# Block owners planned ahead of the places, and the first pair's expert weights issued in another order

## The chip, the cores and the metric

The kernel runs on one core of one Trainium2 chip. The metric is the device time of one execution in microseconds (us). Of several executions the median counts, and a change is judged against the kernel before on the same chip.

## What is computed

The program is a chain of two blocks over 256 tokens of width 1024. The first is a two-layer mixer with a feed-forward network; the second is a mixer followed by a mixture of experts. Only the end of the second block matters here:

```
lg = tok @ rt_g + rt_g_b;  grp = argmax(lg)             # one of 4 groups for each token
le = tok @ rt_e + rt_e_b;  top 2 of the 8 experts in that group
order = argsort(e_flat); counts, starts, padded blocks  # the plan: which expert owns which block
def expert_block(idx, w, e):
    xb = tok_pad[idx]
    hb = silu(xb @ ex_gate[e]) * (xb @ ex_up[e])
    return (hb @ ex_down[e]) * w[:, None]
out = zeros.at[tok_buf].add(y);  x = layernorm(ALPHA * x + g2 * out)
```

There are 32 experts. Each has an input matrix pair (gate and up, 1024 by 512, 2048 KB each) and an output matrix (down, 512 by 1024, 2048 KB), all float32. Which experts are needed, and in what order, is known only once the router has run.

## The kernel before, in words

Each engine has its own program, written out by hand, and the engines meet through semaphores. TensorE is PE, VectorE is DVE, ScalarE is ACT, and SP issues the transfers. The places of the expert blocks are groups of PLACES = 64 token slots. Owned blocks are worked in pairs. There are at most PAIRS = 20 of them, and the loop body runs only for pairs that hold a block.

**Tail** (`tail_vector`, `tail_tensor`, `tail_sync`). DVE routes both token tiles (`route`). As soon as the first tile is routed, the expert of token 0 is known (line 2996), and SP issues that expert's three matrices (line 2746) into the buffers of the pair's second half. PE counts the tokens of every expert (lines 2813 to 2820) and turns the normalised tokens (line 2826); ACT copies them out (line 2872). Then `plan` on DVE works out, from line 3031 to 3050, how many blocks each expert needs, where its blocks end and where they start. From line 3054 on it works out, for both token tiles, the place of each token's two choices (`K.place`, lines 3056 to 3065).

**First block** (`pair_vector`, `pair_tensor`, the part ahead of the loop). One block, that of token 0's expert, is computed while the weights of the first pair are on their way. On DVE this order is written out: `choose` marks the tokens of the first block (lines 3288 and 3292, event `one_chosen`), `owners` computes which expert owns each of 40 blocks (lines 3074 to 3082, event `planned`), `route_weights` works out the routing weights (lines 3013 to 3019), and `weigh` puts them into the block (lines 3302 and 3307). PE waits for `one_chosen`, gathers the block's tokens (line 3126), takes the products with up and gate (lines 3135 and 3136), gathers the first pair's tokens (line 3117), and takes the product with down (line 3160) and the products that put the block's result back on its tokens (line 3169).

**Pair weights** (`pair_sync`). SP waits for `planned`, reads the number of blocks, and in a loop over the pairs reads the two owners and issues six transfers, two gate and up pairs and two down matrices:

```
for unit, sources in (("pair_in", ...), ("pair_down", ...)):
    for j, e in enumerate(experts):
        sp.wait_ge(K.used_up((unit, j)), K.free_count((unit, j), i))
```

[...] Half 0 of a pair lies in three slots of the weight ring, which are free by then. Half 1 lies in three buffers of its own in the arena, and these are the ones that the first block reads: its input matrices until line 3136 is done, its down matrix until line 3160 is done. That there is one buffer set for each half, and no more, ties each transfer to the products of the pair before.

**Loop on PE.** For each pair: input products of half 0, then of half 1 (lines 3184 and 3185), the turned hidden values (line 3196), output products of half 0 (line 3208), the next pair's gather (line 3117), output products of half 1 (line 3208), the rest of the gather, and the products that put the results back (line 3239).

Of the kernel before, what the change touches and what calls it, by code (L numbers as in the profile page):

```python
# [19 lines left out]
P = 128  # L20
# [1369 lines left out]
EXPERTS, GROUPS_E, PER_GROUP, D_EXPERT = 32, 4, 8, 512  # L1390
# [100 lines left out]
PLACES = 64  # L1491
TOP = 2
BLOCKS = (TOP * T + EXPERTS * (PLACES - 1)) // PLACES
PAIRS = -(-BLOCKS // 2)
# [1406 lines left out]
def tail_vector(dve, K):  # L2901
# [47 lines left out]
    for tt in range(TT):  # L2949
        route(dve, K, link, tt)  # L2950
    plan(dve, K, link)
    K.dve_base = link.base + link.n

# [53 lines left out]
def route_weights(dve, K, link, tt):  # L3007

    tt_op, ts_op = dve.tensor_tensor, dve.tensor_scalar
    s = K.rt_s[:, tt, :]  # L3010
    dve.wait_ge(K.sem["rt_e2"], K.count("rt_e2", 0, tt + 1))

    ts_op(s[:, 4:5], s[:, 1:2], 1.0, None, ALU.add).then_inc(link.sem, 1)
    dve.wait_ge(link.sem, link.count())
    tt_op(s[:, 4:5], s[:, 4:5], s[:, 0:1], ALU.mult).then_inc(link.sem, 1)
    dve.wait_ge(link.sem, link.count())
    dve.reciprocal(s[:, 4:5], s[:, 4:5]).then_inc(link.sem, 1)
    dve.wait_ge(link.sem, link.count())
    tt_op(s[:, 5:6], s[:, 4:5], s[:, 1:2], ALU.mult).then_inc(link.sem, 1)
    dve.wait_ge(link.sem, link.count())  # L3020


def plan(dve, K, link):

    tt_op, ts_op, stt = dve.tensor_tensor, dve.tensor_scalar, dve.scalar_tensor_tensor
    dve.wait_ge(K.full(("pos", 0)), K.full_count(("pos", 0)))
    dve.wait_ge(K.full(("total", 0)), K.full_count(("total", 0)))

    total, its = K.bank(("total", 0))[:, 0:EXPERTS], K.bank(("pos", 0))[:, EXPERTS:2 * EXPERTS]
    blocks, ends, first, apart = (K.plan[:, k, :] for k in range(4))  # L3030
    ts_op(blocks, total, 0.0, None, ALU.is_gt).then_inc(link.sem, 1)
    dve.wait_ge(link.sem, link.count())
    for k in range(1, T // PLACES):
        ins = stt(out=blocks, in0=total, scalar=float(k * PLACES), in1=blocks, op0=ALU.is_gt, op1=ALU.add)
        if k < T // PLACES - 1:
            ins.then_inc(link.sem, 1)
            dve.wait_ge(link.sem, link.count())
        else:
            ins.then_inc(K.empty(("total", 0)), 1)
            dve.wait_ge(K.empty(("total", 0)), K.drained_count(("total", 0)))  # L3040
    tt_op(blocks, blocks, its, ALU.subtract).then_inc(link.sem, 1)
    dve.wait_ge(link.sem, link.count())
    dve.tensor_tensor_scan(ends, K.ones[:, 0:EXPERTS], blocks, 0.0, ALU.mult, ALU.add).then_inc(link.sem, 1)
    dve.wait_ge(link.sem, link.count())

    tt_op(first, ends, blocks, ALU.subtract).then_inc(link.sem, 1)
    dve.wait_ge(link.sem, link.count())
    stt(out=apart, in0=first, scalar=-float(PLACES), in1=its, op0=ALU.mult, op1=ALU.mult).then_inc(link.sem, 1)
    dve.wait_ge(link.sem, link.count())
    stt(out=first, in0=first, scalar=1.0, in1=its, op0=ALU.add, op1=ALU.subtract).then_inc(link.sem, 1)  # L3050
    dve.wait_ge(link.sem, link.count())
    for tt in range(TT):
        dve.wait_ge(K.full(("pos", tt)), K.full_count(("pos", tt)))
        pos = K.bank(("pos", tt))[:, 0:EXPERTS]
        t = K.ended[:, 0, :]
        stt(out=K.chosen[:, tt, :], in0=first, scalar=float(PLACES), in1=pos, op0=ALU.mult, op1=ALU.add).then_inc(link.sem, 1)
        stt(out=t, in0=pos, scalar=float(PLACES), in1=apart, op0=ALU.is_lt, op1=ALU.mult).then_inc(K.empty(("pos", tt)), 1)
        dve.wait_ge(link.sem, link.count())
        dve.wait_ge(K.empty(("pos", tt)), K.drained_count(("pos", tt)))
        tt_op(K.chosen[:, tt, :], K.chosen[:, tt, :], t, ALU.add).then_inc(link.sem, 1)  # L3060
        dve.wait_ge(link.sem, link.count())
        for k in range(TOP):
            tt_op(t, K.chosen[:, tt, :], K.rt_hot[:, tt, 1 + k, :], ALU.mult).then_inc(link.sem, 1)
            dve.wait_ge(link.sem, link.count())
            dve.tensor_reduce(K.place[:, tt, k:k + 1], t, AX_X, ALU.add).then_inc(link.sem, 1)
            dve.wait_ge(link.sem, link.count())


def owners(dve, K, link):

    tt_op, ts_op = dve.tensor_tensor, dve.tensor_scalar
    ends = K.plan[:, 1, :]
    n = 2 * PAIRS
    tt_op(K.ended, K.token[:, 0:n].unsqueeze(2).broadcast_to([P, n, EXPERTS]), ends.unsqueeze(1).broadcast_to([P, n, EXPERTS]),
          ALU.is_ge).then_inc(link.sem, 1)
    dve.wait_ge(link.sem, link.count())
    dve.tensor_copy(K.owner[:, n:n + 1], ends[:, EXPERTS - 1:EXPERTS])
    dve.tensor_reduce(K.owner[:, 0:n], K.ended, AX_X, ALU.add).then_inc(link.sem, 1)
    dve.wait_ge(link.sem, link.count())
    ts_op(K.owner[:, 0:n], K.owner[:, 0:n], float(EXPERTS - 1), None, ALU.min).then_inc(link.sem, 1)  # L3080
    dve.wait_ge(link.sem, link.count())
    dve.tensor_copy(K.block_expert[:, 0:n + 1], K.owner[:, 0:n + 1]).then_inc(K.sem["planned"], 1)


def pair_sync(sp, K, A):

    sp.wait_ge(K.sem["planned"], K.count("planned"))
    blocks = block_count(sp, K)
    with sp.Fori(0, PAIRS) as i, sp.If(i * 2 < blocks):
        experts = [sp.value_load(K.block_expert[0:1, bass.ds(i * 2 + j, 1)], min_val=0, max_val=EXPERTS - 1) for j in range(2)]  # L3090
        for unit, sources in (("pair_in", (A["ex_gate_2"], A["ex_up_2"])), ("pair_down", (A["ex_down_2"],))):
            for j, e in enumerate(experts):
                sp.wait_ge(K.used_up((unit, j)), K.free_count((unit, j), i))
                sp.sem_inc(K.sync_steps, 1)
                for a, dst in zip(sources, K.pair_w[unit, j]):
                    k = a.shape[2] // P
                    weights = a[0, bass.ds(e, 1)].rearrange("a (p k) n -> p (a k) n", k=k)
                    sp.dma_start(dst.rearrange("p (k n) -> p k n", k=k), weights).then_inc(K.landed((unit, j)), 16)


def block_count(eng, K):

    eng.wait_ge(K.sem["planned"], K.count("planned"))
    return eng.value_load(K.block_expert[0:1, 2 * PAIRS:2 * PAIRS + 1], min_val=1, max_val=BLOCKS)
# [179 lines left out]
def choose(dve, K, link, at, n, done):  # L3284

    slots = K.token[:, at:at + n]
    for tt in range(TT):
        ins = dve.tensor_scalar(K.hit[:, tt, 0, 0:n], slots, K.place[:, tt, 0:1], None, ALU.is_equal)
    ins.then_inc(link.sem, 1)
    dve.wait_ge(link.sem, link.count())  # L3290
    for tt in range(TT):
        ins = dve.scalar_tensor_tensor(out=K.chosen_at[:, tt, 0:n], in0=slots, scalar=K.place[:, tt, 1:2], in1=K.hit[:, tt, 0, 0:n],
                                       op0=ALU.is_equal, op1=ALU.add)
    ins.then_inc(K.sem[done], 1)
# [31 lines left out]

def pair_vector(dve, K):
    link = Chain(K.place_done)
    choose(dve, K, link, 0, PLACES, "one_chosen")
    more = Chain(K.dve_done, K.dve_base)  # L3330
    owners(dve, K, more)
    for tt in range(TT):
        route_weights(dve, K, more, tt)
    K.dve_base = more.base + more.n
# [30 lines left out]
    blocks = block_count(dve, K)  # L3365
    with dve.Fori(0, PAIRS) as i, dve.If(i * 2 < blocks):
        link = Chain(K.place_done, FIRST_LINKS, i, PLACE_LINKS)
# [326 lines left out]
def program(nc, A, out):  # L3694
# [7 lines left out]
    with ExitStack() as ctx:  # L3702
# [19 lines left out]
        @block.sync  # L3722
        def _(sp):
            for tt, landed in enumerate((K.dma_x, K.dma_x_2)):
                sp.dma_start(K.x_tok[:, tt, :], A["x"][0, tt * P:(tt + 1) * P, :]).then_inc(landed, 16)
            layer_sync(sp, K, A)
            mid_sync(sp, K, A)
            tail_sync(sp, K, A)
            pair_sync(sp, K, A)
            for tt in range(TT):  # L3730
                sp.wait_ge(K.sem["x5"], K.count("x5", 0, tt + 1))
                sp.dma_start(out[0, tt * P:(tt + 1) * P, :], K.x_tok[:, tt, :]).then_inc(K.dma_out, 16)
            sp.wait_ge(K.dma_out, 32)
# [55 lines left out]
```

## Time and profile before

| | us |
|---|---|
| median of 3 runs | 2050.88 (2049.94 to 2054.84) |
| the profiled execution, its own time | 2051.53 |
| its span, first to last instruction | 2049.3 |
| share of the span in which PE is busy | 97% |
| mean granted clock of PE | 0.985 of 2.4 GHz |

The span is read from the first to the last instruction, and times in the rows below are counted from its start. A busy PE is one with a matmul in its pipeline. "Granted clock" is the share of 2.4 GHz that the chip gave PE; 0.50 is 1.2 GHz. A line of idle time names who ended it. The tail runs to about 1576 us, the first block from there to 1607 us, and 14 pairs from there to 2031 us; the last layer norm and the store of the output end the program.

### The profile page before, as it was taken

The numbers are of one execution on the slowest core, as the hardware profiler recorded it, in microseconds if no ns is written. First come the engines' busy times: TensorE is split into PE (matmuls) and PEld (weight loads), VectorE is DVE, ScalarE is ACT, GpSimd is POOL, SyncE is SP. The second block draws the span as 40 slices with busy tenths as digits, with TensorE's granted clock in tenths as the row PEclk, the third lists the DMA queues.
The fourth block names the chain that finished last, engine by engine and source line by source line (L and its number), as shares of the span: only waits on it lengthen the run. The fifth ranks groups of instructions, "written<-read, shape, count | busy, mean of one in ns | idle before, by whom it ended". The sixth has DMA issues, their size and how long they took to land.

```text
span 2049.3 us, 35729 instructions
## 1 busy us (share of the span) xinstructions
PE 1987.9 (97%) x14735; PEld 1371.6 (67%) x14735; DVE 1097.6 (54%) x1847; ACT 477.9 (23%) x902; POOL 250.5 (12%) x233
## 2 busy tenths in 40 slices
PE   8999999999999999999999999999997999999996
PEld 5778869964867868994445565999975444444442
DVE  2685276753569157665578757444547323323324
ACT  3165110001436311000331144433233110111011
POOL 4684000000667100000000011000000000000000
PEclk9999999999999999999999999999996999999998
DMA  8332535554533355536622245100014999999992
GB/s 252 124 124 103 205 124 168 162 195 122 182 123 124 107 201 165 165 126 251 242 82 82 82 149 180 44 4 4 4 46 160 400 414 414 422 413 413 422 413 112
DMA packets 138707, 385.51 MB, mean 188 GB/s; under 512 B 16935, under 2 KB 64399, under 8 KB 127441
## 3 DMA queue, kind: packets, MB, share of 16 engines
q1 hardware_dynamic: 138577, 383.61, 50.4%
q8 instruction: 102, 1.67, 0.3%
q14 instruction: 28, 0.23, 0.0%
HBM read 382.54 MB, written 1.05 MB: 187 GB/s over the span
## 4 chain that ended last, share of the span: by engine, by line
PE 90%; ACT 4%; DVE 4%; issue 2%; DMA 0%; DVEq 0%; SPq 0%; ACTq 0%
PE psum L408 17%; PE psum L666 12%; PE psum L1609 10%; PE psum L3184 9%; PE psum L2352 8%; PE psum L3208 5%; PE psum L709 5%; PE psum L3117 3%; PE psum L426 3%; PE psum L3239 2%; PE psum L725 2%; PE psum L629 2%; PE psum L642 1%; PE psum L1814 1%; ACT arena L1979 1%
## 5 line engine op out<-in xcount | busy, mean ns | idle before, releaser
L408 PE MATMUL psum<-arena,ring 128*128 128x256 f32 x1728 | 382.3, 380 | 1.0 <-ACT arena L776 1.0
L408 PEld LDWEIGHTS psum<-arena,ring 128*128 128x128 f32 x1728 | 324.0, 189 | 55.4 <-issue 8.2
L2352 PE MATMUL psum<-arena 64*64 64x64 f32 (+1 forms) x4320 | 179.9, 237 | 2.7 <-issue 1.5
L2352 PEld LDWEIGHTS psum<-arena 64*64 64x64 f32 x4320 | 171.7, 134 | 4.7 <-issue 2.7
L666 PE MATMUL psum<-arena,ring 128*128 128x128 f32 x1280 | 149.6, 275 | 0.3 <-issue 0.2
L666 PEld LDWEIGHTS psum<-arena,ring 128*128 128x128 f32 x1280 | 146.1, 192 | 0.6 <-issue 0.6
L1609 PE MATMUL psum<-arena,ring 128*128 128x512 f32 (+2 forms) x432 | 142.2, 489 | 0.0
L776 ACT ACTIVATE arena<-psum 128x512 f32<-128x512 f32 (+2 forms) x84 | 44.7, 558 | 380.9 <-PE psum L408 163.0
L1609 PEld LDWEIGHTS psum<-arena,ring 128*128 128x128 f32 (+1 forms) x432 | 80.6, 187 | 61.4 <-issue 55.8
L666 PE MATMUL psum<-arena 128*128 128x128 f32 x960 | 113.7, 274 | 0.0
L666 PEld LDWEIGHTS psum<-arena 128*128 128x128 f32 x960 | 110.4, 192 | 0.0
L3323 DVE TENSOR_TENSOR arena<-psum,arena 64x512 f32<-64x512 f32 x58 | 40.0, 689 | 120.1 <-PE psum L3208 115.3
L2521 ACT ACTIVATE arena<-psum 128x256 f32<-128x256 f32 (+1 forms) x156 | 68.4, 446 | 141.5 <-PE psum L2352 52.9
L3184 PE MATMUL psum<-ring,arena 128*64 128x512 f32 x224 | 99.1, 595 | 0.0
L3185 PE MATMUL psum<-ring,arena 128*64 128x512 f32 x224 | 99.1, 595 | 0.0
L3373 DVE TENSOR_TENSOR arena<-arena,psum 64x512 f32<-64x512 f32 x28 | 19.0, 679 | 149.1 <-ACT arena L3265 149.1
L3185 PE MATMUL psum<-arena 128*64 128x512 f32 x224 | 98.6, 591 | 0.0
L3184 PE MATMUL psum<-arena 128*64 128x512 f32 x224 | 98.6, 591 | 0.0
L2161 DVE SCALAR_TENSOR_TENSOR arena<-psum,arena 128x189 f32<-128x189 f32 (+3 forms) x184 | 80.5, 438 | 21.6 <-ACT arena L1918 13.2
L3184 PEld LDWEIGHTS psum<-ring,arena 128*64 128x64 f32 x224 | 29.5, 137 | 66.6 <-issue 66.6
L3184 PEld LDWEIGHTS psum<-arena 128*64 128x64 f32 x224 | 30.4, 136 | 64.4 <-issue 64.4
L3265 ACT ACTIVATE arena<-psum 64x512 f32<-64x512 f32 x28 | 16.7, 595 | 230.6 <-PE psum L3185 230.6
(464 smaller groups left out, 3051.5 us busy)
## 6 DMA issues: line engine op xcount, KB each, us to landing
ring<-in_w_in_dram SPq DMA_DIRECT2D x29, 2048.0 KB, 8.1
ring<-in_ffn_w_dram SPq DMA_DIRECT2D x46, 1024.0 KB, 7.7
arena<-in_ex_gate_dram SPq DMA_DIRECT2D x15, 2048.0 KB, 11.0
arena<-in_ex_up_dram SPq DMA_DIRECT2D x15, 2048.0 KB, 15.5
arena<-in_ex_down_dram SPq DMA_DIRECT2D x15, 2048.0 KB, 14.8
ring<-in_ex_gate_dram SPq DMA_DIRECT2D x14, 2048.0 KB, 8.1
ring<-in_ex_up_dram SPq DMA_DIRECT2D x14, 2048.0 KB, 12.6
ring<-in_ex_down_dram SPq DMA_DIRECT2D x14, 2048.0 KB, 16.2
```

Source lines behind the costliest of these rows:

```text
L408: ins = pe.matmul(bank[:, j, :], w[:, kc, c * P:(c + 1) * P], moving[:, kc, :], start=kc == 0, stop=kc == k - 1)
L426: ins = pe.matmul(bank, K.xT[:, kc, tt * P:(tt + 1) * P], w[:, kc, :], start=kc == 0, stop=kc == DC - 1)
L666: ins = pe.matmul(bank[:, x, w, :], weights(w)[:, k, :], moving[:, k, :], start=k == 0, stop=k == 3)
L709: ins = pe.matmul(K.bank(key), tokens[:, k, :], weights[:, k, :], start=u == k == 0, stop=key[0] == "p" and u == BY_SEVEN - 1 and k == 1)
L1609: ins = pe.matmul(out, a, b, start=i == 0, stop=i == len(pairs_) - 1)
L2161: last = stt(out=o, in0=i, scalar=w, in1=o, op0=ALU.mult, op1=ALU.add)
L2352: ins = pe.matmul(bank[r, u, :], a[r, u], b[r, u], start=i == 0, stop=i == len(terms) - 1)
L2521: act.activation(dst, src, ACT.Copy).then_inc(K.empty(key), 1)
L3117: ins = pe.matmul(bank[:, u * P:(u + 1) * P], K.x_hat[:, tt, kc * P:(kc + 1) * P], K.chosen_at[:, tt, :], start=tt == 0, stop=tt == TT - 1)
L3184: pe.matmul(bank[0:PLACES, :], K.xg[:, kc, mine], up[:, kc, :], start=kc == 0, stop=kc == DC - 1)
L3185: ins = pe.matmul(bank[PLACES:P, :], K.xg[:, kc, mine], gate[:, kc, :], start=kc == 0, stop=kc == DC - 1)
L3208: ins = pe.matmul(bank[hf * PLACES:(hf + 1) * PLACES, :], K.p_hidT[:, j, kc, :], w[:, kc, hf * BANK:(hf + 1) * BANK], start=kc == 0, stop= ...
```

## The change

On DVE, `plan` is cut in two. Its first part (lines 3023 to 3051) stays where it was, at the end of the tail. Its second part, which computes the places, becomes a function `places`. `pair_vector` now calls `owners`, then `places`, then `choose` for the first block. No instruction of DVE is added or removed.

On SP, the first pair is taken out of the loop, and its six transfers are issued in the order input 0, output 0, input 1, output 1. The loop over the other pairs keeps its order (input 0, input 1, output 0, output 1) and starts at 1.

```diff
@@ plan(dve, K, link), after line 3051
+def places(dve, K, link):
+
+    tt_op, stt = dve.tensor_tensor, dve.scalar_tensor_tensor
+    first, apart = K.plan[:, 2, :], K.plan[:, 3, :]
     for tt in range(TT):
         dve.wait_ge(K.full(("pos", tt)), K.full_count(("pos", tt)))
         ...
@@ pair_sync(sp, K, A)
     sp.wait_ge(K.sem["planned"], K.count("planned"))
     blocks = block_count(sp, K)
-    with sp.Fori(0, PAIRS) as i, sp.If(i * 2 < blocks):
-        experts = [sp.value_load(K.block_expert[0:1, bass.ds(i * 2 + j, 1)], ...) for j in range(2)]
-        for unit, sources in (("pair_in", (A["ex_gate_2"], A["ex_up_2"])), ("pair_down", (A["ex_down_2"],))):
+
+    def owned(i):
+        return [sp.value_load(K.block_expert[0:1, bass.ds(i * 2 + j, 1)], ...) for j in range(2)]
+
+    def load(unit, j, i, e):
+        sp.wait_ge(K.used_up((unit, j)), K.free_count((unit, j), i))
+        sp.sem_inc(K.sync_steps, 1)
+        ...
+            sp.dma_start(dst.rearrange("p (k n) -> p k n", k=k), weights).then_inc(K.landed((unit, j)), 16)
+
+    experts = owned(0)
+    for unit, j in (("pair_in", 0), ("pair_down", 0), ("pair_in", 1), ("pair_down", 1)):
+        load(unit, j, 0, experts[j])
+    with sp.Fori(1, PAIRS) as i, sp.If(i * 2 < blocks):
+        experts = owned(i)
+        for unit in ("pair_in", "pair_down"):
             for j, e in enumerate(experts):
-                ...
+                load(unit, j, i, e)
@@ pair_vector(dve, K)
     link = Chain(K.place_done)
-    choose(dve, K, link, 0, PLACES, "one_chosen")
     more = Chain(K.dve_done, K.dve_base)
     owners(dve, K, more)
+    places(dve, K, more)
+    choose(dve, K, link, 0, PLACES, "one_chosen")
     for tt in range(TT):
         route_weights(dve, K, more, tt)
```

## Rows read from the trace of the kernel before

**Rows 1.** The page: busy time, and the loop's input products (busy, mean ns | idle before).

```profile
PE 1987.9 (97%) x14735; PEld 1371.6 (67%) x14735; DVE 1097.6 (54%) x1847; ACT 477.9 (23%) x902; POOL 250.5 (12%) x233
...
L3184 PE MATMUL psum<-ring,arena 128*64 128x512 f32 x224 | 99.1, 595 | 0.0
```

**Rows 2.** Waits of PE, 1569 to 1608 us (who waited for whom: us, times, longest).

```profile
PE psum L3126 <- DVE arena L3292: 2.9, 1, 2.9
```

**Rows 3.** Timeline of DVE, 1572 to 1580 us (start, us, engine, line, operation).

```profile
1572.13 0.19 DVE L3056 SCALAR_TENSOR_TENSOR arena<-arena,psum 128x32 f32<-128x32 f32 x1
...
1575.62 0.48 DVE L3292 SCALAR_TENSOR_TENSOR arena<-arena 128x64 f32<-128x64 f32 x2
1576.02 1.48 DVE L3074 TENSOR_TENSOR arena<-arena 128x1280 f32<-128x1280 f32 x1
...
1579.34 0.19 DVE L3082 CAST block_expert<-arena 128x41 int32<-128x41 f32 x1
1579.44 0.14 DVE L3013 TENSOR_SCALAR arena<-arena 128x1 f32<-128x1 f32 x1
```

**Rows 4.** Timeline of PE and ACT from the tail's end to the second pair.

```profile
1571.30 3.68 ACT L2872 ACTIVATE arena<-psum 128x512 f32<-128x512 f32 x4 [1.57 <-PE psum L2826]
1576.36 7.01 PE L3126 MATMUL psum<-arena 128*128 128x64 f32 x32 [2.88 <-DVE arena L3292]
1584.11 1.09 PE L3135 MATMUL psum<-arena 128*64 128x512 f32 x1 [0.74 <-issue]
...
1590.09 0.59 PE L3135 MATMUL psum<-arena 128*64 128x512 f32 x1
...
1594.07 3.84 PE L3117 MATMUL psum<-arena 128*128 128x128 f32 x32
...
1599.27 3.66 PE L3160 MATMUL psum<-arena 128*64 128x512 f32 x16 [0.52 <-issue]
...
1607.35 0.64 PE L3184 MATMUL psum<-ring,arena 128*64 128x512 f32 x1
...
1614.27 0.59 PE L3184 MATMUL psum<-arena 128*64 128x512 f32 x1
...
1622.42 3.65 PE L3208 MATMUL psum<-ring,arena 128*64 128x512 f32 x16
1628.61 3.66 PE L3208 MATMUL psum<-arena 128*64 128x512 f32 x16
1637.62 0.64 PE L3184 MATMUL psum<-ring,arena 128*64 128x512 f32 x1
```

**Rows 5.** Timeline of SP's queue: the first pair's transfers being issued.

```profile
1582.09 0.34 SPq L3098 DMA_DIRECT2D ring<-in_ex_gate_dram  x1
1582.53 0.38 SPq L3098 DMA_DIRECT2D ring<-in_ex_up_dram  x1
...
1594.81 0.38 SPq L3098 DMA_DIRECT2D arena<-in_ex_up_dram  x1
1595.39 0.33 SPq L3098 DMA_DIRECT2D ring<-in_ex_down_dram  x1
...
1603.10 0.33 SPq L3098 DMA_DIRECT2D arena<-in_ex_down_dram  x1
```

**Rows 6.** DMA view, a window about each issue: KB, us from issue to landing.

```profile
ring<-in_ex_up_dram SPq DMA_DIRECT2D x1, 2048.0 KB, 13.2
...
arena<-in_ex_up_dram SPq DMA_DIRECT2D x1, 2048.0 KB, 12.5
...
ring<-in_ex_down_dram SPq DMA_DIRECT2D x1, 2048.0 KB, 16.8
...
arena<-in_ex_down_dram SPq DMA_DIRECT2D x1, 2048.0 KB, 14.0
```

**Rows 7.** Windows: length, busy time of each engine, PEclk, DMA share, GB/s.

```profile
1573.00:1576.30 3.30, 0.48 (x4) 0.24 (x2) 2.89 (x15) 1.98 (x3) 0.00 (x0) 1.00 1.04 447
1576.40:1590.00 13.60, 12.86 (x46) 8.68 (x48) 6.81 (x24) 1.89 (x2) 0.00 (x0) 0.50 0.75 294
1590.10:1607.30 17.20, 15.86 (x82) 8.24 (x78) 5.15 (x10) 2.33 (x5) 0.00 (x0) 1.00 0.92 366
...
1608.00:1640.00 32.00, 31.89 (x157) 13.56 (x154) 10.61 (x25) 3.51 (x7) 0.00 (x0) 1.00 0.99 416
```

More of the change, by code:

```diff
@@ L3088, in pair_sync @@
     blocks = block_count(sp, K)
-    with sp.Fori(0, PAIRS) as i, sp.If(i * 2 < blocks):
-        experts = [sp.value_load(K.block_expert[0:1, bass.ds(i * 2 + j, 1)], min_val=0, max_val=EXPERTS - 1) for j in range(2)]
-        for unit, sources in (("pair_in", (A["ex_gate_2"], A["ex_up_2"])), ("pair_down", (A["ex_down_2"],))):
-            for j, e in enumerate(experts):
[L3093 to L3098, printed above, removed]
+    def owned(i):
+        return [sp.value_load(K.block_expert[0:1, bass.ds(i * 2 + j, 1)], min_val=0, max_val=EXPERTS - 1) for j in range(2)]
+    def load(unit, j, i, e):
+        sp.wait_ge(K.used_up((unit, j)), K.free_count((unit, j), i))
+        sp.sem_inc(K.sync_steps, 1)
+        sources = (A["ex_gate_2"], A["ex_up_2"]) if unit == "pair_in" else (A["ex_down_2"],)
+        for a, dst in zip(sources, K.pair_w[unit, j]):
+            k = a.shape[2] // P
+            weights = a[0, bass.ds(e, 1)].rearrange("a (p k) n -> p (a k) n", k=k)
+            sp.dma_start(dst.rearrange("p (k n) -> p k n", k=k), weights).then_inc(K.landed((unit, j)), 16)
[5 more added lines that the diff above has]
+        for unit in ("pair_in", "pair_down"):
+            for j, e in enumerate(experts):
+                load(unit, j, i, e)
 def block_count(eng, K):
```

## The prediction

> **What bounds the kernel now.** I read the page first, then the waits of PE, then the timeline around the place of the change, then the DMA rows. The page says that PE is busy for 97% of the span, and that the input products of the pair loop, 224 matmuls of line 3184 on the ring's weights, had 0.0 us of idle time ahead of them [rows 1]. So PE never stood waiting for a pair's weights. The loop's period says the same: the first pair starts at 1607.35 us and the second at 1637.62, 30.27 us later [rows 4], and PE is busy for 31.89 of 32 us about there. The DMA engines are nearly full in that stretch too, a share of 0.99 [rows 7]. That is worth a look, because a full DMA could be the real pace. What decides it is whether weights land before or after they are wanted, and they land well before, as counted below.
>
> Ahead of the loop PE has one real wait: line 3126, the gather of the first block, waits 2.9 us for DVE's line 3292, the last instruction of `choose` [rows 2]. The other thing that it needs, ACT's copies of the turned tokens, ends at 1571.30 + 3.68 = 1574.98 [rows 4]. DVE ends at 1575.62 + 0.48 = 1576.10 [rows 3], and PE starts at 1576.36. From there PE goes on to the loop with gaps under a microsecond. So in the stretch that the change touches the path runs: DVE's plan, places, choose, then PE to the end.
>
> **The change part by part.**
>
> *Owners moved ahead of places and choose.* In the trace `owners` starts at 1576.02 (line 3074) and the next function starts at 1579.44 (line 3013): 3.42 us from start to start, two large instructions of 1.5 us each and small ones [rows 3]. Today it runs after `one_chosen`, beside PE's gather, and costs the path nothing. Moved, it stands where line 3056 stands now (1572.13), and everything behind it up to `choose` moves back by 3.42 us. ACT's copies end at 1574.98, too early to cover any of it: DVE is already 1.12 us behind them. So `one_chosen` comes at 1576.10 + 3.42 = 1579.52, and the gather starts at 1579.78. Cost: **+3.42 us** on the path.
>
> *What is queued behind on DVE.* `route_weights` and `weigh` keep their absolute time, since owners merely passed from behind choose to ahead of it. PE wants the weighted block only after the gather at line 3117, which starts at 1594.07 [rows 4]. The second `choose` waits for the gather itself and moves with it, and so do ACT's copies. Cost nothing, gain nothing.
>
> *`planned` earlier.* It is signalled at 1579.34 + 0.19 = 1579.53 now, and at 1572.13 + (1579.53 - 1576.02) = 1575.64 then: 3.89 us sooner [rows 3]. SP took 1582.09 - 1579.53 = 2.56 us from there to its first issue [rows 5]. Taking the first pair out of the loop leaves the same loads of owners and drops the loop's entry. I take 2.56 again; the bounds are 0 and twice that, and neither reaches PE, as follows.
>
> *Do earlier weights release anybody?* Four deadlines of the first pair, landing against first use:
> - input 0: up issued at 1582.53, landed 13.2 us later, 1595.7; used at 1607.35. Margin 11.6.
> - input 1: up issued at 1594.81, landed at 1607.3; used at 1614.27. Margin 7.0.
> - output 0: issued at 1595.39, landed at 1612.2; used at 1622.42. Margin 10.2.
> - output 1: issued at 1603.10, landed at 1617.1; used at 1628.61. Margin 11.5 [rows 4 to 6].
>
> Every margin is positive, so the expected gain of the SP part is **0**. The change widens the margins of input 0 (about 3.9 + 3.4 = 7.3 us more) and of output 0, which no longer stands behind SP's wait for the first block's input buffers. It does not widen the tightest, input 1: that issue waits for line 3136 of the first block, which itself moves back by 3.42 us, so landing and use both move. The extra 2048 KB ahead of it are gone by then: at the loop's 416 GB/s [rows 7] three transfers of 2048 KB take 3 x 5.0 us, and from an issue at 1578.2 they are through by about 1595, before input 1 is issued at 1598.2. In later pairs each transfer waits for PE to be done with its buffer, so those move with PE.
>
> *Contention.* Input 0 now starts at 1578.2, while the tail of the first block's down matrix may still be in flight. That matrix is wanted at line 3160, now 1599.27 + 3.42 = 1602.7. A full input pair in front of it costs under 13.2 us, which it can stand. Cost nothing.
>
> *TensorE's clock.* The granted clock was 1.00 (2.4 GHz) from 1573.0 to 1576.3, while PE had next to nothing to do; 0.50 (1.2 GHz) from 1576.4 to 1590.0; and 1.00 after [rows 7]. So the gather and part of lines 3135 and 3136 run slowly. Seven pairs of them took 1590.09 - 1584.11 = 5.98 us, 0.85 each, and the other nine took 1594.07 - 1590.09 = 3.98, 0.44 each [rows 4]: 0.41 us for each pair that runs at the other level. My sum assumes that the low stretch ends after the same seven pairs, because what PE does behind its idle time is the same sequence, moved.
>
> [...]
>
> **The sum.** +3.42 us on DVE, 0 on SP, 0 for the clock. The profiled execution (2051.53) would become 2054.95. It stands 0.65 above the median of the runs, so I forecast 2050.88 + 3.42 = 2054.3, 0.17% more. A measurement of this kernel can tell about 0.3%, 6.15 us, from no change: bounds 2044.7 and 2057.0. The forecast falls inside.
>
> **The rivals.**
>
> *A: the clock turns on the longer idle time (slower).* PE's idle time ahead of line 3126 grows from 2.88 to 6.30 us. If the clock then rises later by more than the shift, the nine fast pairs run at 0.85: + 9 x 0.41 = 3.7, sum 7.1, 2058.0. If the gather at line 3117 (3.84 us for 32 matmuls) is slow too, it takes about the 7.01 us of line 3126's 32: 3.2 more, 2061.2. It passes the bound of 0.3% from the seventh extra slow pair on ((6.15 - 3.42) / 0.41 = 6.7). For it: the clock did fall after an idle stretch at this place. Against: behind the idle time there is the same dense work, which brought it back within seven pairs. Chance 0.14 beyond the bound.
>
> *B: the clock gives some back (same).* If the rise stays at 1590.1 in time while PE's chain moves, line 3135 starts at 1587.5 and only three pairs are slow, 4 x 0.41 = 1.6 back: 2052.7. If gather and products all ran at the high level, 3.2 + 7 x 0.41 = 6.1 would come back: 2048.2. No row favours that, since the clock fell at 1576.4 while PE was still near idle. Chance 0.15, all of it inside 0.3%.
>
> *C: the weights were the pace (faster).* If the nearly full DMA set the loop's start, 3.89 us of earlier issue and one transfer (5.0 us) out of the way would bring up to 8.9 us: 2042.0. Against it stand 0.0 us of idle time ahead of the loop's products and four positive margins. Chance 0.03.
>
> *D: the order does not change in fact.* DVE and SP run in program order, as these timelines show, so the moved instructions must move. Under 0.01; 2050.9.
>
> **How the numbers follow.** Forecast 0.67, A 0.14, B 0.15, C 0.03, D 0.01. Same within 0.3% is the forecast, B and D: 0.83. Slower is A: 0.14. Faster is C: 0.03. The range runs from D's 2050.9, which takes in B's first case less the 0.9 us by which the lowest run lay under the median, to A's first case with the 0.7 us by which the profiled execution lay above it: 2050.9 to 2058.7. It leaves out C, B's extreme and A with a slow gather, under 0.2 in all.
>
> **What would show it right or wrong.** On DVE: line 3074 right behind line 3050, and line 3292 of the first block ending about 1579.5. On PE: 6.3 us of wait at the gather in place of 2.9, the first pair at about 1610.8 in place of 1607.35, and the period still 30.27. On SP: first issue about 1578.2, then ring down about 1579.2, then the arena pair held back until about 1597.8. In the page, line 3184 still with 0.0 us of idle time. It would be wrong if the first pair started before 1609 with the clock unchanged, or if the period fell below 30.27, which would mean that the weights had been the pace after all. A low clock reaching into line 3117 would make it rival A.

## The result and the profile after

| | before | changed |
|---|---|---|
| median of 20 runs each, us | 2053.02 (2049.33 to 2057.56) | 2055.09 (2053.41 to 2058.66) |
| ratio | 1 | 1.0017, 95% interval 1.0011 to 1.0023 |
| span of the profiled execution | 2049.3 | 2052.3 |
| mean granted clock | 0.985 | 0.986 |

The change makes the kernel slower, by less than the 0.3% that was set as the bound: 1.0017 is 3.5 us, with 2.3 to 4.7 us in the interval. That ratio comes from all 40 runs and is not the quotient of the two medians, which is 1.0010 (2.07 us); the means are 2.75 us apart. So the times say that the change costs some 2 to 4 us, and no more exactly than that; where the cost arises is read from the traces. Later runs were made on other chips, each beside runs of the kernel before on the same chip; their ratios are to those.

In the changed kernel the line numbers from line 3052 on are higher: `owners` is 3080 to 3088, places 3062 to 3071, `choose` 3305 and 3309, the gather 3143 (was 3126), up and gate 3152 and 3153 (were 3135 and 3136), the pair's gather 3134 (was 3117), and the loop's input products 3201 and 3202 (were 3184 and 3185). The timeline of DVE, changed kernel, answers to [rows 3]:

```profile
1572.67 0.19 DVE L3050 SCALAR_TENSOR_TENSOR arena<-arena,psum 128x32 f32<-128x32 f32 x1
1572.89 1.49 DVE L3080 TENSOR_TENSOR arena<-arena 128x1280 f32<-128x1280 f32 x1
...
1576.22 0.19 DVE L3088 CAST block_expert<-arena 128x41 int32<-128x41 f32 x1
1576.32 0.18 DVE L3062 SCALAR_TENSOR_TENSOR arena<-arena,psum 128x32 f32<-128x32 f32 x1
...
1579.80 0.48 DVE L3309 SCALAR_TENSOR_TENSOR arena<-arena 128x64 f32<-128x64 f32 x2
```

`owners` stands right behind line 3050 and takes 1576.32 - 1572.89 = 3.43 us from start to start. Everything behind it moved by that. The timeline of PE, changed kernel, against [rows 4]:

```profile
1570.05 0.64 PE L2819 MATMUL psum<-arena 128*128 128x32 f32 x2 [2.86 <-DVE arena L3002]
...
1580.54 7.06 PE L3143 MATMUL psum<-arena 128*128 128x64 f32 x32 [5.95 <-DVE arena L3309]
1588.33 1.09 PE L3152 MATMUL psum<-arena 128*64 128x512 f32 x1 [0.74 <-issue]
...
1591.77 0.70 PE L3152 MATMUL psum<-arena 128*64 128x512 f32 x1
...
1597.15 3.84 PE L3134 MATMUL psum<-arena 128*128 128x128 f32 x32
...
1610.43 0.64 PE L3201 MATMUL psum<-ring,arena 128*64 128x512 f32 x1
...
1617.34 0.59 PE L3201 MATMUL psum<-arena 128*64 128x512 f32 x1
...
1640.69 0.64 PE L3201 MATMUL psum<-ring,arena 128*64 128x512 f32 x1
```

Two traces are set against each other best from a point that both have and that the change doesn't touch. That is line 2819, the counts of the second token tile, which started at 1569.29 in the trace of before and at 1570.05 here; the 0.76 us between them arose further up. From there the gather came 1576.36 - 1569.29 = 7.07 us later before, and 1580.54 - 1570.05 = 10.49 us later now: **3.42 us**, the first term of the sum. From the gather to the first pair it is 1607.35 - 1576.36 = 30.99 us before and 1610.43 - 1580.54 = 29.89 now: 1.10 us came back. 0.76 + 3.42 - 1.10 = 3.08, and the spans differ by 3.0. The period is 1640.69 - 1610.43 = 30.26, as before.

In these two traces the 1.10 us are the clock's: a pair is one matmul of line 3152 and one of 3153, and here four pairs are slow and one lies between the levels, where there were seven slow ones (from start to start a pair took 0.85 us at the granted clock of 0.50 and 0.43 at 1.00). The windows of the changed kernel (columns as in [rows 7]):

```profile
1575.00:1578.30 3.30, 0.00 (x0) 0.00 (x0) 2.85 (x13) 0.78 (x1) 0.00 (x0) 1.00 1.04 447
1578.40:1591.90 13.50, 10.62 (x42) 8.14 (x44) 5.48 (x28) 1.89 (x2) 0.00 (x0) 0.50 1.01 431
1592.00:1610.40 18.40, 17.06 (x87) 8.55 (x84) 5.18 (x10) 2.33 (x5) 0.00 (x0) 1.00 0.84 335
```

The low stretch is as long as before, but PE worked for only 10.62 us of it, against 12.86: it begins at 1578.4, 2.1 us ahead of the gather, so 2.1 us of it now fall on PE's wait, where they cost nothing.

SP's queue of the changed kernel, and the landings of its ring up, arena up and ring down transfers, against [rows 5, 6]:

```profile
1578.44 0.34 SPq L3106 DMA_DIRECT2D ring<-in_ex_gate_dram  x1
1578.87 0.38 SPq L3106 DMA_DIRECT2D ring<-in_ex_up_dram  x1
1579.45 0.33 SPq L3106 DMA_DIRECT2D ring<-in_ex_down_dram  x1
...
1597.88 0.38 SPq L3106 DMA_DIRECT2D arena<-in_ex_up_dram  x1
```

```profile
ring<-in_ex_up_dram SPq DMA_DIRECT2D x1, 2048.0 KB, 12.5
...
arena<-in_ex_up_dram SPq DMA_DIRECT2D x1, 2048.0 KB, 12.4
...
ring<-in_ex_down_dram SPq DMA_DIRECT2D x1, 2048.0 KB, 16.8
```

Input 0 landed at 1591.4 and was used at 1610.43: its margin grew from 11.6 to 19.1 us. Input 1 landed at 1610.3 and was used at 1617.34: 7.1 us, as before. The weights came earlier, and nobody had been waiting for them.

### The profile page after: what moved, and what is told of

Same layout as the page of the kernel before. It is cut to its first block, busy times and chain, and to the rows that moved or that the text cites. A ratio compares the mean times of both kernels' runs of the same rounds, so it can differ in the third digit from the quotient of the medians.

```text
span 2052.3 us, 35720 instructions
## 1 busy us (share of the span) xinstructions
PE 1986.0 (97%) x14735; PEld 1371.4 (67%) x14735; DVE 1098.6 (54%) x1847; ACT 477.6 (23%) x902; POOL 248.8 (12%) x233
## 4 chain that ended last, share of the span: by engine, by line
PE 90%; ACT 4%; DVE 4%; issue 2%; DMA 0%; POOL 0%; DVEq 0%; SPq 0%; ACTq 0%; POOLq 0%
PE psum L408 17%; PE psum L666 12%; PE psum L1609 10%; PE psum L3201 9%; PE psum L2352 8%; PE psum L3225 5%; PE psum L709 5%; PE psum L3134 3%; PE psum L426 3%; PE psum L3256 2%; PE psum L725 2%; PE psum L629 2%; PE psum L642 1%; PE psum L2768 1%; PE psum L1814 1%
## 5 line engine op out<-in xcount | busy, mean ns | idle before, releaser
L2161 DVE SCALAR_TENSOR_TENSOR arena<-psum,arena 128x189 f32<-128x189 f32 (+3 forms) x184 | 80.5, 439 | 21.6 <-ACT arena L1918 13.2
```

Source lines behind the costliest of these rows:

```text
L2161: last = stt(out=o, in0=i, scalar=w, in1=o, op0=ALU.mult, op1=ALU.add)
```

## The experiments

Three numbers are taken from every trace: A, from line 2819's start (or what stands for it) to the gather's; B, from the gather's start to the first pair's; C, from the gather's start to the end of the last matmul. A grows when the gather comes later, B when the first block runs more slowly, and C takes in the pair loop too. Each A, B and C is from one trace. Each ratio is to the kernel before on the same chip and comes from all the timed runs (20 and 20 for the changed kernel, 4 to 11 and 21 to 24 for the others), so it can differ by about 0.1% from the quotient of the medians. "SP new" is the changed kernel's order of the first pair, "SP old" the order of before. The last line is a second trace of the kernel before.

| kernel | A | B | C | ratio (95%) |
|---|---|---|---|---|
| before | 7.07 | 30.99 | 454.79 | 1 |
| changed | 10.49 | 29.89 | 453.60 | 1.0017 (1.0011 to 1.0023) |
| SP part alone | 7.07 | 29.35 | 453.06 | 1.0008 (0.9999 to 1.0017) |
| DVE part alone | 10.50 | 29.50 | 453.31 | 1.0026 (1.0015 to 1.0038) |
| owners twice | 14.04 | 30.95 | 454.66 | 1.0046 (1.0032 to 1.0060) |
| input 0 late, DVE old | 7.07 | 39.15 | 465.62 | 1.0072 (1.0056 to 1.0087) |
| places batched, SP new | 6.07 | 29.35 | 453.15 | 0.9999 (0.9989 to 1.0008) |
| PE filled, SP new | 8.15 | 24.73 | 449.56 | 0.9989 (0.9980 to 0.9998) |
| filled, batched, SP new (first fill) | 6.42 | 25.61 | 451.87 | 0.9980 (0.9971 to 0.9989) |
| before, filled | 7.06 | 24.81 | 448.60 | 0.9978 (0.9969 to 0.9987) |
| change, filled | 11.26 | 24.73 | 448.54 | 0.9992 (0.9981 to 1.0002) |
| batched, filled, SP old | 6.96 | 24.74 | 448.53 | 0.9962 (0.9948 to 0.9976) |
| batched, filled, SP new | 5.47 | 24.80 | 450.14 | 0.9969 (0.9959 to 0.9980) |
| before again | 7.11 | 31.20 | 457.28 | (one run) |

### One part at a time

The SP part alone: the changed kernel, with DVE in the old order.

```diff
     more = Chain(K.dve_done, K.dve_base)
-    owners(dve, K, more)
     places(dve, K, more)
     choose(dve, K, link, 0, PLACES, "one_chosen")
+    owners(dve, K, more)
```

> The SP part alone: the first pair taken out of the loop and issued input 0, output 0, input 1, output 1; DVE keeps the order places, choose, owners. Theory (PE waits for DVE's choose, never for a pair's weights): ratio 1.000, the gather starts 0.26 us behind the last instruction of choose as before, wait of PE there 2.9 us, first issue of SP about 2.5 us behind planned, the three ring transfers in a row, first pair about 31 us after the gather's start, period 30.27. Rival C (weights are the pace): 0.1% to 0.4% faster. A rival that the new order costs the loop something (input 1 late behind output 0): slower, and the first products on the arena's weights would show a wait.

The DVE part alone: the changed kernel, with `pair_sync` of before (all pairs in the loop, input, input, output, output).

> The DVE part alone: owners, then places, then choose; SP issues the first pair in the loop as before. Theory: all of the change's cost is here, +3.42 us at the gather's start, ratio 1.0017 (1.0011 to 1.0023), wait of PE at the gather about 5.9 to 6.3 us. Rival: the cost comes from the SP part or from both together, then this would be under 1.001.

The traces give the whole of A to the DVE part: A is 7.07 without the DVE part and 10.50 with it. Waits of PE from 1572 to 2030 us, first the SP part alone, then the DVE part alone:

```profile
PE psum L3143 <- DVE arena L3309: 2.5, 1, 2.5
PE psum L3186 <- issue: 0.8, 1, 0.8
PE psum L3152 <- issue: 0.7, 1, 0.7
PE psum L3177 <- issue: 0.5, 1, 0.5
```

```profile
PE psum L3132 <- DVE arena L3298: 6.1, 1, 6.1
```

Below this line the DVE part alone has three lines of "issue" of the same sizes. No line names a DMA. The ratios are weaker evidence. That of the DVE part holds 1.0017 within its interval; that of the SP part holds both no change and 1.0017. So that the SP part is free rests on A, on the waits and on the period (1638.03 - 1607.76 = 30.27), not on its times. No gain of rival C's size is seen: 0.1% faster lies outside the interval.

The SP part alone did use up something that no wait shows. It issues output 0 ahead of input 1, and without the earlier `planned` the three transfers into the ring go out at 1583.62 to 1584.63, 5.2 us later than in the changed kernel. Input 1's issue, its landing, and its first use:

```profile
1595.21 0.38 SPq L3106 DMA_DIRECT2D arena<-in_ex_up_dram  x1
```

```profile
arena<-in_ex_up_dram SPq DMA_DIRECT2D x1, 2048.0 KB, 16.7
```

```profile
1614.68 0.59 PE L3201 MATMUL psum<-arena 128*64 128x512 f32 x1
```

The transfer took 16.7 us where it took 12.5 before, and the margin is 1614.68 - 1611.9 = 2.8 us in place of 7.0. In the changed kernel it is 7.1: there the ring's transfers had been issued earlier and the last of them landed at 1596.3, ahead of input 1's issue at 1597.88; here it was issued at 1584.63, took 17.4 us and landed at 1602.0, 6.8 us behind input 1's issue.

### Does the clock answer to a longer wait?

`owners` computed twice ahead of places, the second time over the first. With `last=False` it does not signal `planned`; the lines for that are left out here.

```diff
     more = Chain(K.dve_done, K.dve_base)
+    owners(dve, K, more, last=False)
     owners(dve, K, more)
     places(dve, K, more)
```

> The changed kernel with owners computed twice ahead of places (the second time over the first). Theory: the gather starts another 3.42 us later, so 6.84 over the kernel before, ratio about 1.0033, and the time from the gather's start to the first pair stays within 29 to 32 us, whatever the clock's phase. Rival A (the clock answers to the longer idle time): PE now stands about 9.4 us ahead of the gather; if the low stretch grows with it, the time from the gather's start to the first pair grows by 3 us or more, ratio 1.005 or above. Rival B (the clock rises at a fixed time): that stretch shrinks by 1.6 us more, ratio 1.0025.

```profile
PE psum L3148 <- DVE arena L3314: 9.8, 1, 9.8
```

```profile
1573.30:1576.60 3.30, 0.46 (x4) 0.22 (x2) 3.16 (x6) 1.99 (x3) 0.00 (x0) 1.00 1.07 457
1576.70:1597.00 20.30, 12.66 (x46) 8.81 (x48) 9.76 (x42) 1.89 (x2) 0.00 (x0) 0.50 0.89 360
1597.20:1614.50 17.30, 15.96 (x82) 8.24 (x78) 5.16 (x10) 2.33 (x5) 0.00 (x0) 1.00 0.74 292
```

These are its wait at the gather and its windows. A grew by 6.97 us over before, twice the cost of `owners`. The low stretch did grow, from 13.6 to 20.3 us, but PE's busy time within it is 12.66, against 12.86 in the kernel before [rows 7]: most of the growth fell on the wait and not on the work. Against the changed kernel's 10.62 it is 2.0 us more, and B is 1.06 more. The four traces with a wait of under 3 us and no fill or late transfer have B from 29.35 to 31.20, so one trace cannot tell whether that 1.06 is the longer wait's. B is 30.95, inside the 29 to 32 of the theory. Rival A asked for a B at least 3 us longer, and the trace does not show it. The ratio, 1.0046, is 9.4 us (6.6 to 12.3); the theory's 6.84 lies at its lower edge, and whether a part of the rest is the clock's in other executions stays open.

### Were the weights ever close?

The SP part alone (DVE in the old order), with the first pair issued input 1, input 0, output 0, output 1. Input 1 must wait for the first block to be done with its buffers, and input 0 stands behind it in SP's program.

```diff
-    for unit, j in (("pair_in", 0), ("pair_down", 0), ("pair_in", 1), ("pair_down", 1)):
+    for unit, j in (("pair_in", 1), ("pair_in", 0), ("pair_down", 0), ("pair_down", 1)):
```

> DVE in the order of before; the first pair's transfers issued input 1, input 0, output 0, output 1, so that input 0 is issued only when the first block is done with input 1's buffers (about 13 us after its issue in the kernel before, whose margin was 11.6, and behind 2 x 2048 KB). Theory (weights have a margin and only that hides them): issue at about 1595.2, landing at about 1617 in the clock of the trace of before, first pair held to about 1617 in place of 1607.35, so about 10 us slower, ratio 1.005, up to 3 us more if the low clock follows the new idle time; a wait for the DMA at the first products of the ring's weights, and only there. Rival C (the DMA's pace sets the loop): the loop's period changes too, above or below 30.27. If PE did not need them at all: ratio 1.000.

SP's issues, then PE's first pair and the second one's start:

```profile
1593.04 0.38 SPq L3106 DMA_DIRECT2D arena<-in_ex_up_dram  x1
...
1594.11 0.48 SPq L3106 DMA_DIRECT2D ring<-in_ex_up_dram  x1
```

```profile
1615.41 1.11 PE L3201 MATMUL psum<-ring,arena 128*64 128x512 f32 x1 [9.78 <-DMA ring<-in_ex_up_dram]
...
1648.35 0.64 PE L3201 MATMUL psum<-ring,arena 128*64 128x512 f32 x1
```

SP held input 0 back with input 1. `planned` came at 1579.25 + 0.19 = 1579.44 (line 3088), and the next transfer issued is input 1's gate, at 1592.61, 13.2 us behind it, with input 0 behind that: its up matrix went out 1594.11 - 1569.19 = 24.92 us behind line 2819, against 1584.05 - 1571.34 = 12.71 with the SP part alone, where nothing stands ahead of it.

The wait of 9.78 us is what the margins gave (about 10). It shows too that the view of waits does name a DMA where one is late, so that its silence in the other kernels counts. The next period is 32.94 us in place of 30.27, once, since the clock was low from 1607.2 to 1620.8 and that stretch reached from the wait into the pair's products: 2.7 us. That looks like rival A at another place, but it is not shown to be the wait's: two other traces, shown below, have a low stretch as their first pair begins (2.3 and 2.5 us) without such a wait. Together 12.5 us; the ratio says 14.8 (11.5 to 17.9).

### A shorter way to the gather

SP as in the changed kernel, the old order on DVE, and the products and sums of places for both token tiles and both choices at once. The semaphores and the first two products are left out here.

```diff
-        tt_op(K.chosen[:, tt, :], K.chosen[:, tt, :], t, ALU.add)
-        for k in range(TOP):
-            tt_op(t, K.chosen[:, tt, :], K.rt_hot[:, tt, 1 + k, :], ALU.mult)
-            dve.tensor_reduce(K.place[:, tt, k:k + 1], t, AX_X, ALU.add)
+    tt_op(K.chosen, K.chosen, t, ALU.add)
+    tt_op(both, K.chosen.unsqueeze(2).broadcast_to([P, TT, TOP, EXPERTS]), K.rt_hot[:, :, 1:1 + TOP, :], ALU.mult)
+    dve.tensor_reduce(K.place.rearrange("p t k -> p (t k)"), K.ended[:, 4:4 + TT * TOP, :], AX_X, ALU.add)
```

> A candidate: SP as in the changed kernel, DVE in the order of before (places, choose, owners), and places computed for both token tiles and both choices at once, 7 instructions in place of 14. Theory: from line 3056 of before to choose 3.04 us shrink to about 1.5, but ACT's copies of the turned tokens end 1.12 us ahead of choose and then end last, so the gather starts 1.1 us earlier than before and not 1.5, and the ratio is 0.9995 to before. A rival (the clock takes it back): the gather starts earlier and the first pair does not.

```profile
1571.42 3.70 ACT L2872 ACTIVATE arena<-psum 128x512 f32<-128x512 f32 x4 [1.57 <-PE psum L2826]
...
1573.46 0.29 DVE L3073 TENSOR_REDUCE arena<-arena 128x4 f32<-128x128 f32 x1
1573.79 0.42 DVE L3307 TENSOR_SCALAR arena<-arena 128x64 f32<-128x64 f32 x2
...
1575.48 5.88 PE L3145 MATMUL psum<-arena 128*128 128x64 f32 x32 [1.76 <-ACT arena L2872]
```

In this timeline DVE is done with places at 1573.75, 1.53 us from line 3062's start at 1572.26 to `choose`, where it took 3.04. But ACT's copies end at 1571.42 + 3.70 = 1575.12, and PE's wait now names them, so A fell by 1.00 us and not by 1.5, as expected. A gain of 1 us is beyond what the ratio can tell.

### What the clock costs there

PE is given matmuls without use while it waits. In the kernel before:

```diff
+    pe.wait_ge(K.empty(("h2", 0, 0)), K.empty_count(("h2", 0, 0)))
+    for _ in range(3):
+        pe.matmul(K.bank(("h2", 0, 0))[:, 0:T], K.ones, K.token, start=True, stop=True)
     pe.wait_ge(K.sem["route"], K.count("route", 0, 2))
@@ at the start of pair_tensor
+    pe.wait_ge(K.empty(("first", 1)), K.empty_count(("first", 1)))
+    for _ in range(7):
+        pe.matmul(K.bank(("first", 1))[:, 0:T], K.ones, K.token, start=True, stop=True)
```

The first two tries had 5 and 12, and 5 and 8 of them, and the bank of the gather in place of `first`. Both have DVE's order of before and SP's order of the change, and the second has places batched too.

> The SP part alone, and PE given matmuls without use (256 columns, constant operands, into banks that are overwritten afterwards) while it waits: 5 before the second route's counts, 12 before the gather. Tests how much of the time from the gather to the first pair is the low clock. Theory: that stretch (29.35, 29.5, 29.9, 30.95, 30.99 us so far, with 3 to 7 slow pairs) becomes 24 to 25 us with the gather and all 16 pairs at 2.4 GHz (3.4 us less for the gather's 32 matmuls, 0.41 us less for each slow pair), while the gather starts within 0.5 us of where it did; ratio 0.997 to 0.998. Rival (this stretch is set by something other than the clock, or a wait of any length brings it low): it stays at 29 to 31 us, ratio 1.000.

> The last one with places batched as in the earlier candidate (5 and 8 matmuls without use). Theory: 5 to 6 us from the clock, and about 1 us from the earlier gather, ratio 0.9965 to 0.9975, faster than both kernels. Rival: the matmuls without use push the gather back by what the batching won; then as with PE filled alone.

B fell to 24.73 us in the first, as expected. But the fill was too long: there A is 8.15, and the five matmuls ahead of the counts ran over their wait as well. PE began the counts 1570.19 - 1568.91 = 1.28 us after DVE's line 3005 had started, against 1569.29 - 1569.04 = 0.25 in the kernel before (line 3002 there), and A, which starts at the counts, does not see that 1.0 us. So the gather was 2.1 us late in all, and 0.8 us of the second kernel's gain was lost in the same way. And the first of the two showed a wait that no kernel had had:

```profile
1610.96 0.64 PE L3207 MATMUL psum<-arena 128*64 128x512 f32 x1 [0.80 <-DMA arena<-in_ex_up_dram]
```

With the stretch 6 us shorter and output 0 ahead of it, input 1 of the first pair is no longer early: its up matrix was issued at 1590.52 and landed 20.3 us later, at 1610.8. The second one's clock fell once more at 1600.2, to 0.50 for 6.7 us, so its C is 3.3 us above 448.5 while its B shows only 0.9 of that; the rest is in its first period, 32.73 us. A second trace of the kernel before, run beside them, shows such a fall too, at 1603.8, and a first period of 32.55 us:

> The kernel before once more, for a second trace. Theory: from the second route's counts (line 2819) to the gather 7.07 us as before; from the gather to the first pair anywhere from 29.3 to 31 us, as the clock falls. If it is 30.99 again, the difference of 1.1 us to the changed kernel's trace is the change's own.

```profile
1545.80:1586.70 40.90, 32.54 (x135) 27.72 (x135) 29.84 (x111) 14.92 (x33) 0.00 (x0) 0.50 0.52 201
1586.80:1603.70 16.90, 15.56 (x84) 8.33 (x81) 4.17 (x9) 2.33 (x5) 0.00 (x0) 1.00 0.96 389
1603.80:1610.50 6.70, 6.70 (x15) 1.79 (x15) 3.25 (x9) 0.00 (x0) 0.00 (x0) 0.50 1.02 435
```

B is 31.20 and C is 2.5 us above that of the first trace, of the same kernel. So B and C move by some microseconds from one execution to the next, and the 1.10 us that the changed kernel's trace gave back are within that: they are no property of the change that one trace could show.

Then four kernels with 3 matmuls ahead of the counts and another number ahead of the gather, on one chip: the kernel before (3 and 7), the whole change (3 and 14), and places batched with SP in the old and in the new order (3 and 5).

> The kernel before, with matmuls without use while PE waits (3 ahead of the second route's counts, 7 ahead of the gather, sized so that they end before the wait does). Theory: the gather starts where it did (7.07 us behind line 2819's start, up to 0.3 more), the clock is high from then on, the gather to the first pair takes 24.7 us as with the fill before, and as output 0 is not issued ahead of input 1 here, the first products on the arena's weights do not wait. Ratio 0.997 to 0.998. Rival: 3 in place of 5 matmuls ahead of the counts do not bring the clock up, then the gather stays slow and the ratio is about 1.000.

> The whole change with the same fill (3 and 14, for the longer wait). Tells whether the change pays once the clock's loss is gone and the weights' margin has shrunk. Theory: the gather starts 3.4 us later than in the filled kernel before, the weights come in time in both, so this kernel is about 3.4 us slower than that one, ratio to the kernel before 0.999 to 1.000. Rival C in a new form (with the clock high the weights are the pace and the change pays): as fast as the filled kernel before or faster.

> Candidate: fill (3 and 5), places batched, SP in the order of before. Theory: the gather 1.0 us earlier than before, 24.7 us to the first pair, no wait for weights: about 6 to 7 us off, ratio 0.9965 to 0.9975; up to 3 us less gain in executions where the clock falls once more behind the first block's small products.

> The last one with SP in the changed order (input 0, output 0, input 1, output 1). Theory: output 0's 2048 KB (about 4.9 us of the DMA engines) stand ahead of input 1, whose margin is smaller with the clock high, so PE waits 0.5 to 2 us for the arena's up matrix in the first pair, once; slower than the same kernel with the old order by that much, too little to see in the ratio, but plain in the waits. Rival: no wait, the order is free.

Windows of the filled kernel before, then its gather; under them the wait of the last kernel in the list:

```profile
1558.60:1568.70 10.10, 9.29 (x35) 7.94 (x35) 7.22 (x39) 4.47 (x14) 0.00 (x0) 0.50 0.56 202
1568.80:1600.00 31.20, 27.79 (x159) 17.64 (x159) 17.46 (x61) 7.95 (x11) 0.00 (x0) 1.00 0.91 373
```

```profile
1575.19 3.75 PE L3132 MATMUL psum<-arena 128*128 128x64 f32 x32 [1.33 <-DVE arena L3298]
```

```profile
1607.61 0.64 PE L3209 MATMUL psum<-arena 128*64 128x512 f32 x1 [1.33 <-DMA arena<-in_ex_up_dram]
```

The gather takes 3.75 us in place of 7.01, and from its start to the first use of input 1, 1575.2 to 1606.9, the granted clock is 1.00. The filled kernel before is 0.9978. The filled change is 0.9992: its median is 2.5 us above that of the filled kernel before (2049.48 and 2046.95), its mean 3.4, where 3.4 were expected; A differs by 4.2, as 14 matmuls ran over the wait by 0.8. The intervals of the two ratios overlap from 0.9981 to 0.9987, but C is the same (448.54 and 448.60) and A is longer, so with a high clock the change wins nothing either. It comes closer to being needed: in the filled kernel before, input 1 lands at 1587.45 + 16.8 = 1604.25 us and is used at 1606.91, a margin of 2.7 left of 7.0; in the filled change 4.4 are left.

Three matmuls ahead of the counts did not always bring the clock up. Line 2826 (2829 in these kernels), 16 matmuls, took 1.95 and 1.94 us in the filled kernel before and in the last one, but 3.65 in the filled change and in the batched kernel with the old order. In that batched kernel the granted clock was 0.50 from 1566.0 to 1574.7, so the fill ahead of the gather began at the low clock as well, at 1574.74, and ran past the end of `choose` at 1575.72; the gather started at 1577.38, so A is 6.96 and not the 6 that was expected. Where the clock was up (0.97 from 1568.9 to 1574.3 in the last kernel), ACT's copies ended earlier too, 5.02 us behind the counts' start in place of 5.71 in batching alone, and A is 5.47, below the 6.07 there.

With DVE's old order and the fill, the new order of SP costs something. In the last kernel output 0 stands ahead of input 1, whose up matrix lands 20.8 us after its issue, and PE waits 1.33 us for it. C says the same: 450.14 against 448.53. The 1.49 us that this kernel's A is ahead are the clock's, as just said, so A and C together are equal (455.61 and 455.49). The intervals of the two ratios overlap, so the times alone don't show it. The batched kernel with the old order, 0.9962 (0.9948 to 0.9976), is faster than both kernels of this case; its gain over the filled kernel before is not resolved by the intervals.

## Why the prediction was right

*Owners on the path, +3.42 us.* Right to the hundredth in the traces: A grew by 3.42, by 3.43 with the DVE part alone, and by 6.97 with `owners` twice. Without the DVE part the cost is gone (A 7.07).

*ACT's copies cannot cover it.* Right. They ended 1.1 us ahead of DVE, and batching places won 1.00 us and stopped there.

*What is queued behind on DVE, 0.* Right: line 3013 starts 10.15 us behind line 2819 in both traces (1579.44 - 1569.29 before, 1580.20 - 1570.05 now).

*SP's part worth 0.* Right in the trace. The margins came out as worked out: 19.1 us for input 0 (11.6 + 7.3 = 18.9) and 7.1 for input 1 (7.0). From `planned` to the first issue SP took 1578.44 - 1576.41 = 2.03 us, not 2.56; nothing hangs on it. The step that output 0 is "gone by then" rests on the earlier `planned`, and it held only together with it: with the SP part alone input 1's margin was 2.8 us, and with a filled PE and DVE's old order PE waited 0.80 and 1.33 us for it. The prediction weighed the order only within the whole change, where it is free (margins of 7.1 us, and 4.4 filled).

*The clock, 0.* This term was the weak one. I took "the same seven pairs" as slow; the trace has four and one between, 1.10 us less. The sign is rival B's, and the size is near its 1.6. But the second trace of before moved B and C by up to 2.5 us without any change, so a single value was not to be had; a term with a spread of two microseconds either way would have been the honest one. Rival A, that a longer wait makes more of the work slow, did not come true at this place with waits of 6 and 9.8 us, one trace each. Where a wait of 9.78 us came ahead of the pair loop, 2.7 us were lost to a low clock, but 2.3 and 2.5 us were lost there in two traces without that wait, so its cause stays open. With PE kept busy it took 24.7 to 24.8 us to the first pair in five of the six filled kernels and 25.6 in the sixth, against 29.4 to 31.2 in those that neither fill nor hold a transfer back; but in one trace PE was busy for 32.54 of 40.90 us and the clock was 0.50 all the same. And the count of slow pairs varies for one and the same kernel: of the two traces of the kernel before one has seven, the other four and one between the levels.

*The sum.* 3.42 us forecast, 3.5 (2.3 to 4.7) measured. That the two agree to 0.1 us is luck: the interval is 2.4 us wide, and the medians differ by 2.07. The forecast of the time itself, 2054.3, is 0.8 us below the median, and that is luck too, for two errors partly cancel: the kernel before was 2.1 us slower in 20 runs than in the three shown, and the medians rose by 1.35 less than the 3.42.

## What to carry to other kernels

Earlier issue of a transfer was worth nothing here while its margin (landing to first use) was positive: the four were 7.0 to 11.6 us in the kernel before, input 0's grew to 19.1 in the changed kernel, no wait named a DMA in either, and the period stayed at 30.27 and 30.26 us. So count the margins first, then ask what the earlier issue costs the engine that has to enable it. Here that was two big DVE instructions of 1.5 us each, 3.42 us with the small ones, put ahead of the one that PE waited for. Count them for each part of a change alone as well: one part can use up a margin that another gives (input 1's was 2.8 us with the SP part alone and 7.1 with both). Once something else is made faster the margins shrink (7.0 to 2.7 in the kernel before, once filled), and an order of transfers that was free has a price (PE waited 0.80 and 1.33 us); count them again after each change.

## What the runs showed of the hardware

A low clock about an idle stretch cost more here than the wait itself: with a wait of under 3 us at the gather, the stretch from the gather to the first pair took 29.4 to 31.2 us, and 24.7 to 25.6 with PE kept busy in that wait and in the 2.9 us ahead of the counts. The two waits were always filled together, so what each fill does alone is not shown; but in two of the six kernels the clock was still 0.50 after the first fill (the 16 matmuls behind it took 3.65 us in place of 1.94), and the stretch took 24.7 us all the same. Work alone did not bring it back at once: PE was busy for 32.54 of 40.90 us at 0.50 in the second trace of the kernel before, and for all of 6.70 us at 0.50 as its first pair began. Why the clock fell there, behind busy work, stays open. I had also not expected one and the same kernel to differ by 2.5 us from the gather to the end in two executions; it is as large as most of what was measured here.
